# Hybrid attention step on one Trainium2 core: logits two heads ahead, exponentials one head ahead in a third buffer, and an index search that starts from mean and deviation

## What is computed

```python
s = einsum('bthd,bsd->bths', qi, ki)                    # 8 index heads of width 32
score = einsum('bth,bths->bts', wi, relu(s))
score = where(visible, score, -inf)                     # chunk-causal, chunks of 64
top_val, top_idx = lax.top_k(score, top_k)              # 256 prompt, 144 sample
logits = einsum('btjgd,btnjd->btjgn', qg, k_sel) * HEAD_DIM ** -0.5   # 8 heads
p = softmax(where(valid, logits, -inf)); o = einsum('btjgn,btnjd->btjgd', p, v_sel)
# memory: 4 heads over 256 memory tokens, softmax, values
```

## Time and profile before

| quantity | value |
|---|---|
| median of 3 runs (lowest to highest) | 3575.22 us (3574.49 to 3578.63) |
| the profiled execution's own time | 3577.81 us |
| its span, first to last instruction | 3576.0 us |
| mean granted TensorE clock over the span | 0.929 of full |
| busy over the span: PE, PEld, DVE, ACT, POOL | 3084.5, 2868.3, 2205.3, 1062.0, 1261.6 us |

### The profile page before, as it was taken

One profiled execution on the slowest core, in us unless ns is written; L12 is line 12 of the kernel. 1 busy time (PEld: TensorE's weight loads), 2 busy tenths in 40 slices (PEclk: granted clock), 3 DMA queues, 4 the chain that ended last, 5 costly groups with the idle time before them and its releaser, 6 DMA issues. The chain is left out here.

```text
span 3576.0 us, 49691 instructions
## 1 busy us (share of the span) xinstructions
PE 3084.5 (86%) x18810; PEld 2868.3 (80%) x18810; DVE 2205.3 (62%) x4136; ACT 1062.0 (30%) x1812; POOL 1261.6 (35%) x478
## 2 busy tenths in 40 slices
PE   3898994677778886886989999999888999999997
PEld 2777773566666775775989999999888999999996
DVE  4576672576868888863066666666512676667654
ACT  2222221444455664553122122112121212212211
POOL 0000001455666775411453343343214444434420
PEclk8999995688889997998989999999998999999998
DMA  4122225222121110003221111111132111111101
GB/s 137 70 81 78 89 84 138 56 57 57 29 57 29 29 29 26 23 14 99 78 71 36 35 59 47 35 47 47 49 103 89 36 47 59 35 35 59 47 12 50
DMA packets 164759, 201.53 MB, mean 56 GB/s; under 512 B 27759, under 2 KB 138644, under 8 KB 162580
## 3 DMA queue, kind: packets, MB, share of 16 engines
q1 hardware_dynamic: 164628, 199.86, 17.6%
HBM read 154.57 MB, written 45.25 MB: 56 GB/s over the span
## 5 line engine op out<-in xcount | busy, mean ns | idle before, releaser
L877 POOL TENSOR_TENSOR att_relu<-att_relu,keep_w 128x2048 f32<-128x2048 f32 (+12 forms) x84 | 255.5, 3041 | 923.0 <-ACT att_relu L1030 922.5
L1666 DVE SCALAR_TENSOR_TENSOR ffn_gv<-ffn_up,ffn_taps,ffn_gv 128x1056 f32<-128x1056 f32 (+2 forms) x264 | 417.7, 1596 | 143.0 <-ACT ffn_gv L1619 136.7
L1687 DVE TENSOR_TENSOR feed_hT<-feed_hT,ffn_ps_d 128x352 f32<-128x352 f32 x528 | 275.3, 522 | 328.4 <-PE ffn_ps_d L1572 328.4
L1559 PE MATMUL ffn_ps_u<-feed_nhi,feed_up_hi 128*128 128x352 f32 x2112 | 460.1, 326 | 15.9 <-DVE feed_nlo L1697 11.2
L1559 PE MATMUL ffn_ps_u<-feed_nhi,feed_up_lo 128*128 128x352 f32 x2112 | 456.7, 324 | 0.0
L1559 PE MATMUL ffn_ps_u<-feed_nlo,feed_up_hi 128*128 128x352 f32 x2112 | 456.0, 324 | 0.0
L1559 PEld LDWEIGHTS ffn_ps_u<-feed_nhi,feed_up_hi 128*128 128x128 f32 x2112 | 361.0, 190 | 19.7 <-DVE feed_nlo L1697 12.9
L1572 PE MATMUL ffn_ps_d<-ffn_a_hi,ffn_down_hi 128*128 128x352 f32 x1056 | 343.7, 326 | 29.3 <-DVE ffn_a_lo L1678 23.9
L1559 PEld LDWEIGHTS ffn_ps_u<-feed_nhi,feed_up_lo 128*128 128x128 f32 x2112 | 363.6, 188 | 0.0
L1559 PEld LDWEIGHTS ffn_ps_u<-feed_nlo,feed_up_hi 128*128 128x128 f32 x2112 | 360.0, 188 | 0.0
L1572 PE MATMUL ffn_ps_d<-ffn_a_lo,ffn_down_hi 128*128 128x352 f32 x1056 | 343.0, 325 | 0.0
(11 more groups left out here) (248 smaller groups left out, 6030.8 us busy)
## 6 DMA issues: line engine op xcount, KB each, us to landing
feed_raw_up<-in_w_up SPq DMA_DIRECT2D x44, 1024.0 KB, 5.0
scratch_sT<-proj_sT SPq DMA_DIRECT2D x16, 1472.0 KB, 5.1
ffn_raw_down<-in_w_down SPq DMA_DIRECT2D x22, 1024.0 KB, 4.9
feed_nlo<-scratch_mixT SPq DMA_DIRECT2D x16, 528.0 KB, 7.7
proj_x<-in_x_prompt SPq DMA_DIRECT2D x16, 512.0 KB, 4.7
att_qi<-scratch_sT SPq DMA_DIRECT2D x16, 512.0 KB, 3.8
att_qa<-scratch_sT SPq DMA_DIRECT2D x16, 512.0 KB, 5.0
att_qb<-scratch_sT SPq DMA_DIRECT2D x32, 256.0 KB, 5.6
```

Of the source, the lines that this page charges most:

```text
L877: st.step(pool.tensor_tensor(at, at, weights, ALU.mult))
L1559: ins = pe.matmul(ps_u[:, half, s, 0:SUB], a[:, q, k, :], b[:, k, SUB * s:SUB * s + SUB], start=(k == 0 and n == 0), stop=(k == KC - 1 and ...
L1666: ins = dve.scalar_tensor_tensor(gv[:, half, lo:hi], up[:, lo + shift + j - 2:hi + shift + j - 2], taps[:, 2 * j + half, e:e + 1], gv[:, h ...
L1687: dve.tensor_tensor(at, at, ps_d[:, j % 2, 0:SUB], ALU.add).then_inc(partial_read[j % 2], 1)
```

## The change

Logits and masked maxima are made two heads ahead of the head whose values are multiplied, instead of one; exponentials stay one head ahead, but now come first in ACT's slot instead of last, and `probs` has three buffers. PE no longer waits for the memory exponentials before the next block's logits: DVE copies the memory logits from PSUM to `probs`, and ACT works in place there. PE turns two groups before the first multiply, and the index pieces of a slot lie between the groups. The index pieces of a block are spread evenly over nine slots and start three slots earlier. The pick starts one slot earlier (in the last slot of the block before the previous one's end) and has 14 parts in eight slots; its threshold search starts at mean plus a tabled normal quantile times the deviation, and halves eight times from a step of 0.55 deviations, instead of eleven times from half of the range. In DVE's slot the divisions come before the masking. SP loads one more table.

```diff
-HALVINGS = 11
+HALVINGS = 8
+BRACKET = 0.55
+SQRT_SEED = 532487669.0
-        probs = m.sb("probs", [P, 2, SEQ])
+        probs = m.sb("probs", [P, 3, SEQ])
-        SHARE = 10
+        INDEX_LEAD = 3
+        SPREAD = ((0, 1), (2, 3), (4, 5), (6, 7), (8, 9), (10,), (11,), (12, 13))
+        def index_share(slot):
+            b = ahead(BLOCKS[0], (slot + INDEX_LEAD) // NHEADS + 2)
+            if b is None:
+                return None, []
+            total, part = IH * len(b.segs), (slot + INDEX_LEAD) % NHEADS
+            return b, list(range(total * part // NHEADS, total * (part + 1) // NHEADS))
+        def pick_share(slot):
+            b, part = ahead(BLOCKS[0], (slot + 1) // NHEADS + 1), (slot + 1) % NHEADS
+            return b, SPREAD[part] if b and part < len(SPREAD) else ()
...
+            sp.dma_start(quantiles[:, :], t["quantiles"]).then_inc(tables_loaded, 16)
             load(BLOCKS[1])
...
@@ segment_logits (PE)
-                if h == 0 and s < 2 and b.n:
-                    pe.wait_ge(exp_done, NHEADS * b.n)
@@ head_values (PE); rest holds the later segments of the head two ahead
-                turn(0)
+                for g in range(min(2, len(groups))):
+                    turn(g)
                 for g in range(len(groups)):
-                    if g + 1 < len(groups):
-                        turn(g + 1)
-                    if g == 0:
-                        index_pieces(other, numbers)
                     if rest:
                         segment_logits(*rest.pop(0))
                     ins = multiply(g)
+                    if g + 2 < len(groups):
+                        turn(g + 2)
+                    index_pieces(other, numbers[g:g + 1])
...
@@ the loop over slots (PE)
+            for slot in range(-INDEX_LEAD, 0):
+                index_pieces(*index_share(slot))
+            for first_heads in heads[0:2]:
+                early_logits(*first_heads)
+            for i, b, h, _, later in slots():
+                if later:
+                    early_logits(*later)
+                other, numbers = index_share(i)
+                index_pieces(other, numbers[0:2])
                 if h == 0 and b.n:
                     rows_turned(BLOCKS[b.n - 1])
-                head_values(b, h, other, late, after)
+                head_values(b, h, other, numbers[2:], later)
@@ exponentials (ACT), memory head
-                act.wait_ge(turned, last_group(seq - 2) + 1)
                 for mh in range(MH):
-                    ins = act.activation(probs[0:T, seq % 2, 256 * mh:256 * mh + 256], ps_l[...],
-                                         ACT.Exp, bias=neg[0:T, u, 8 + mh:9 + mh], accum_out=...)
+                    row = probs[0:T, seq % 3, MT * mh:MT * mh + MT]
+                    ins = act.activation(row, row, ACT.Exp, bias=neg[0:T, u, 8 + mh:9 + mh], accum_out=...)
@@ pick (DVE), part 0
-                    dve.tensor_reduce(col(low), row, AX.X, ALU.min)
-                    st.step(dve.tensor_reduce(col(mids), row, AX.X, ALU.max))
+                    dve.memset(col(mids), FAR)
+                    for s, (lo, hi) in enumerate(b.segs):
+                        last = dve.bn_stats(stats[0:T, s, :], row[:, lo:hi])
+                    st.step(last)
...
-                    st.step(dve.tensor_scalar(col(spread), col(mids), col(low), None, ALU.subtract))
-                    st.step(dve.tensor_scalar(steps[0:T, :], halves[0:T, :], col(spread), None, ALU.mult))
-                    st.step(dve.tensor_scalar(col(mids, 1), col(mids), col(steps), None, ALU.subtract))
+                    st.step(dve.bn_aggr(moments[0:T, :], stats[0:T, 0:len(b.segs), :].rearrange("p s n -> p (s n)")))
+                    st.step(dve.tensor_scalar(col(sigma).bitcast(I32), col(moments, 1).bitcast(I32), 0.5, SQRT_SEED, ALU.mult, ALU.add))
+                    st.step(dve.tensor_scalar(steps[0:T, :], halves[0:T, :], col(sigma), None, ALU.mult))
+                    st.step(dve.tensor_scalar(col(mids, 1), col(quantiles, b.n), col(sigma), col(moments), ALU.mult, ALU.add))
@@ mask_logits (DVE)
+                if part == 0 and seq >= 3:
+                    dve.wait_ge(turned, last_group(seq - 3) + 1)
...
+                    dve.tensor_copy(probs[0:T, seq % 3, 0:MH * MT].rearrange("p (a n) -> p a n", a=2), ps_l[0:T, :, :]).then_inc(masked, 1)
@@ the loop over slots (DVE)
+            pick(BLOCKS[1], 0)
+            for first_heads in heads[0:2]:
+                mask_logits(*first_heads, 0)
+            for i, b, h, _, later in slots():
                 if h == 0 and b.n:
                     divide(BLOCKS[b.n - 1], 2)
                 if h in (4, 8):
                     divide(b, h // GQ - 1)
+                coming, parts = pick_share(i)
+                if later:
+                    mask_logits(*later, 0)
+                for part in parts[0:1]:
+                    pick(coming, part)
+                if later:
+                    mask_logits(*later, 1)
+                for part in parts[1:]:
+                    pick(coming, part)
@@ constants; normal_quantile inverts the normal distribution on the host
-    halves = np.broadcast_to(f(0.5) ** np.arange(1, HALVINGS + 1, dtype=f), (P, HALVINGS))
+    halves = np.broadcast_to(f(BRACKET) * f(0.5) ** np.arange(HALVINGS, dtype=f), (P, HALVINGS))
+                quantiles[r, n] = normal_quantile(1 - (b.keep - 4.5) / seen)
```

More of the change, by code:

```diff
@@ L14 @@
+import math
 import numpy as np
@@ L947, in turn_group, with head_values @@
                 ins.then_inc(turned, 1)
-            def head_values(b, h, other, numbers, after):
+            def head_values(b, h, other, numbers, later):
                 u, T = b.n % 2, b.T
@@ L979, in multiply @@
                     return ins
-                rest = [(*after, s) for s in range(2, len(after[0].segs))] if after and after[1] < NH else []
-                turn(0)
+                rest = [(*later, s) for s in range(2, len(later[0].segs))] if later and later[1] < NH else []
+                for g in range(min(2, len(groups))):
+                    turn(g)
                 for g in range(len(groups)):
-                    if g + 1 < len(groups):
-                        turn(g + 1)
-                    if g == 0:
-                        index_pieces(other, numbers)
                     if rest:
@@ L1003, in _ @@
             pe.wait_ge(keys_loaded, 16 * KEY_LOADS)
-            early_logits(BLOCKS[0], 0)
-            for b, h, after in slots():
-                other = ahead(b, 2)
-                numbers = portion(other, h) if other else range(0)
-                late = numbers[-1:] if h else range(0)
-                if after:
-                    early_logits(*after)
-                index_pieces(other, numbers[:len(numbers) - len(late)])
+            for slot in range(-INDEX_LEAD, 0):
[7 more added lines that the diff above has]
+                index_pieces(other, numbers[0:2])
                 if h == 0 and b.n:
                     rows_turned(BLOCKS[b.n - 1])
-                head_values(b, h, other, late, after)
+                head_values(b, h, other, numbers[2:], later)
             rows_turned(BLOCKS[NB])
@@ L1047, in _, with relu_next @@
                 index_relu(b, range(IH * len(b.segs)))
-            exponentials(BLOCKS[0], 0)
-            for b, h, after in slots():
-                other = ahead(b, 2)
-                numbers = portion(other, h) if other else range(0)
-                early = len(numbers) - (1 if h and numbers else 0)
-                if other:
-                    index_relu(other, numbers[:early])
+            for slot in range(-INDEX_LEAD, 0):
+                index_relu(*index_share(slot))
+            exponentials(*heads[0])
+            for i, b, h, after, _ in slots():
+                if after:
+                    exponentials(*after)
                 if h == 0 and b.n:
                     copy_groups(act, BLOCKS[b.n - 1], 9)
-                copy_groups(act, b, h, (lambda: index_relu(other, numbers[early:])) if other else None)
-                if after:
-                    exponentials(*after)
+                other, numbers = index_share(i)
+                def relu_next(count, other=other or b, numbers=numbers):
+                    index_relu(other, numbers[:count])
+                    del numbers[:count]
+                copy_groups(act, b, h, relu_next)
             copy_groups(act, BLOCKS[NB], 9)
@@ L1228, in _ @@
                     divide(b, h // GQ - 1)
-                if h < 8 and not b.sample:
-                    pick(ahead(b, 1), 2 * h)
-                if after:
-                    mask_logits(*after, 1)
-                if h < 8 and not b.sample:
-                    pick(ahead(b, 1), 2 * h + 1)
+                coming, parts = pick_share(i)
[7 more added lines that the diff above has]
+                    pick(coming, part)
             divide(BLOCKS[NB], 2)
@@ L1820, in program, with normal_quantile @@
         store_conv(nc, t, ident, hist)
+def normal_quantile(share):
```

(5 more changed lines are left out.)

64 lines of the change are left out of this document (30 added, 34 removed).

## The result

| | before | after |
|---|---|---|
| median of 4 runs each, us | 3576.07 (3574.49 to 3578.63) | 3515.06 (3512.60 to 3517.95) |
| profiled execution, span | 3577.81, 3576.0 | 3515.56, 3513.8 |
| blocks 1 to 14 of the attention | 912.1 | 852.0 |

The ratio is 0.983 (95% interval 0.9818 to 0.9842): 61 us faster, where 115 were forecast. The time is 55 us above the forecast and nearer to the 3525 that the port rule gave. It lies inside the 3392 to 3530 that was to hold 8 in 10, but 5 us beyond the forecast's own 3415 to 3510: only the part of the range that was borrowed from rival 2 holds it.

A forecast was written before the change was run, and what follows sets the result against it. Inner slots were taken as bound by DVE with PE 4% behind, the rest lost at block edges. The terms summed to -115 us from 3577.8, less 2.6 for the median: 3460 us, 8 in 10 within 3392 to 3530.

The forecast's parts named there:

- the port rule: Each mask write on DVE could lose one whole GpSimd instruction at the shared port: 84 us instead of 19, sum 3525.
- rival 2: Two `ps_l` banks keep PE's edges as long as now and POOL's wait half becomes PE's: 3547 us, chance 0.16.
- three halvings: Three fewer threshold halvings in each of 15 blocks, in DVE slots without a gap, taken whole: -92 us.
- start of the pick: On DVE, two reductions go, while statistics per segment and two small steps per block come: net -11 us.
- memory copy: 17 DVE copies of 128x1024 from PSUM to SBUF, priced at the like-shaped mask instruction: +21 us.
- wait for POOL's scores: At block starts, earlier index pieces remove most of DVE's 68.1 us wait, about 10 kept: -58 us.
- edges -28: At block edges, DVE's 56.4 us of waits for PE's logits are halved: -28 us.
- what takes the place +60: Engines share slots less evenly, PE stalls at unit 0; some 4 us come back per block over 15: +60 us.
- blocks 0, 15, 16: Half of the few idle stretches in the last two blocks saved, nothing in the first: -7 us.
- POOL beside DVE: Mask writes already lose 19 us beside POOL; its larger share of time adds 3, left in the range.
- The first: Engines fit better, nothing comes back and waits at edges vanish: 3362, more likely 3375 to 3400 us; chance 0.15.
- The third: A threshold misses its bracket, so blocks run `take_largest`, 91 us each; two such blocks give 3620 us; chance 0.03.

The follow-up runs named there:

- quarters: Changed kernel with each POOL weighting and first sum split into four instructions and the second sum into two: 3467.80 us.
- values first: Changed kernel with each group's multiplies on PE put ahead of the held logit segment: 3506.50 us; with POOL's instructions also cut, 3453.79.
- the search one part later, the fastest run: Changed kernel with POOL's instructions cut, multiplies ahead of held logits, and the search's parts moved by one place: 3444.86 us.

## Why the prediction was off by half

| term | forecast, us | measured, us | from |
|---|---|---|---|
| three halvings | -92 | -90 | L1110 and its small steps and reads, 322.6 to 232.6 |
| start of the pick | -11 | -14 | reductions 41.0 out; statistics, aggregate and root 26.9 in |
| memory copy | +21 | +21 | 17 at 1.213 |
| wait for POOL's scores | -58 | -67 | 68.1 to 0.6 |
| waits for PE: edges -28, what takes the place +60 | +32 | +51 | 56.4 to 107.8 |
| blocks 0, 15, 16 | -7 | 0 | +6, -6, 0 |
| POOL beside DVE | 0, 3 in the range | +40 | 23 to 63 |
| sum | -115 | -59 | profiled executions: -62 |

The measured column adds up because VectorE's busy time and its waits fill the stretch. It says where the time stands; what caused it is for the runs to show.

**Right.** 120 halvings at the old price; the wait for POOL gone; none on the memory exponentials; statistics at 606 ns (22.1 us against 24); three extra mask writes; the inner heads h = 1 to 3 of block 11 still at 6.9 us. Two signs failed: block 11 at 67 us (76.8), and h = 0, which takes 9.5 us with DVE waiting 2.6 of them for PE. That the earlier index pieces take POOL's wait away is shown by undoing them (+60).

**The step that failed** is "POOL beside DVE": "POOL's share of the stretch would rise from 59% to about 67% (536 over 800), which adds 3; I leave that in the range". I scaled the old loss with POOL's share of the time, and took the mask write as the only instruction concerned. In the trace it is a meeting of single instructions: what counts is which of DVE's stand beside which of POOL's, and the change moved both. The marking, for which the prediction has no port price at all, gave 19 of the 40 (26.1 to 45.4), the write 17, an eight-column step 4. Cutting POOL's instructions shows it: 30 and 51 us off the port, 33 and 47 off the time, the whole miss but 8 (11 of the 51 are what the kernel before lost already). That the marking pays could have been read in the trace of before, by single shapes: 1408 columns took longer than 1536.

```profile
L1106 DVE SCALAR_TENSOR_TENSOR att_work<-att_work,att_scores 128x1408 f32<-128x1408 f32 x1 | 3.2, 3206 | 0.0
L1106 DVE SCALAR_TENSOR_TENSOR att_work<-att_work,att_scores 128x1536 f32<-128x1536 f32 x1 | 1.8, 1754 | 0.0
```

The Trainium skill (SBUF — State Buffer, Who interferes with whom) covers the marking too, "A DVE instruction with two SBUF inputs contends with a GpSimd instruction that reads SBUF", and says the form with an accumulator does not. The trace agrees with both: 1.741 to 3.029 for the one, and 1.431 before and after for the halvings. I had read the rule for the mask write only, and then left its 3525 outside the sum and without a chance of its own.

**The term that was mis-sized** is the waits for PE, +51 for +32. The runs do not put it down to the port: with quarters PE's waits behind masks fall from 138 to 99 us, but VectorE's waits for PE stay, at 109.6. Each half of the change alone raises them as much: over 600 to 1700 us these waits are 128 us before and 184 after, 192 with the new search spread in the old order, and 202 with the old search in the new order. They fall with PE's order and the layout of the search: 96.5 in blocks 1 to 14 with quarters and values first, 78.7 with the search one part later as well. The waits with quarters alone:

```profile
DVE att_probs L1221 <- PE att_ps_l L946: 76.2, 62, 4.6
DVE att_inv L1231 <- PE att_ps_o L994: 19.0, 10, 3.6
DVE att_neg L1209 <- PE att_ps_l L932: 14.4, 14, 2.2
```

So the -28 and +60 together were too small by 19, and no run takes apart what that hangs on. In block 11 the working also left out the second mask of h = 7 (1.08 us at 1217.04). One bound is off and enters nothing else: by the row that it names, the low end of the copy is 10 and not 12.

**Luck in the sum.** "They stand in slots where DVE has no gap, so I take them whole" came out at -90 as busy time, but the halvings are not worth that by themselves. In the old order the same search gave +28 or -29 according to its layout. The terms are bound to one another, and a sum of them holds for the whole change only. That 3515 fell inside the range is luck in part: the room came from rival 2, and most of it was filled by the port.

**The rivals.** The second (two PSUM banks keep the edges) forecast 3547, and its sign came true: PE's wait behind masks rose by 54 us, past the 52.6. But the quarters, which leave the banks as they are, take 47 of the 55 us back. How much of the waits for PE that stay hangs on the banks is open, since no run gives `ps_l` more of them. The first (nothing takes the place, 3375 to 3400) is not reached even by the fastest run, 3445. The third did not occur: the mask was written 18 times, as before.

## What to carry to other kernels

Before an instruction is moved beside work on GpSimd, list which of VectorE's instructions take the shared port (here a mask write from SBUF to SBUF and one with two SBUF inputs), and price each at the rest of the GpSimd instruction that it may meet, not at a share of the time. Long GpSimd instructions are then a cost for VectorE: cut in four they cost 62 us more on GpSimd and took 47 off the time, but only in the order in which GpSimd had slack; where it was on the path, the same edit lost 12. And test the halves of a change apart: here the order alone lost 70 us, the search alone lost 28 or gained 29 by its layout over the slots, and both together gained 61.

## What the runs showed that I had not expected

An instruction of eight columns waits as well as one of 1664: the step at L1106 took 1.64 us at 1223.53 in block 11, where it takes 0.23 with quarters. It ended at 1225.17, when POOL's weighting did.

```profile
1221.76 3.39 POOL L889 TENSOR_TENSOR att_relu<-att_relu,keep_w 128x1920 f32<-128x1920 f32 x1 [8.17 <-ACT att_relu L1042]
...
1223.53 1.64 DVE L1106 TENSOR_SCALAR att_steps<-att_halves,att_sigma 128x8 f32<-128x8 f32 x1
```

And POOL pays as well: its second sum of 896 columns took 2.09 us undisturbed, 3.62 behind the marking and 2.74 behind the mask write.

PE's own time fell without fewer matmuls: 695.3 us before, 649.0 after, 624.0 in the fastest run, at a mean granted clock of 0.86, 0.90 and 0.95. Right behind the stall of 2.12 us that ended at 1191 the clock was 0.66 over 5 us, between its two levels of 1.2 and 2.4 GHz (0.5 and 1), and it was 1.00 over the undisturbed 1160 to 1180. The eight transposes there took 1.91 us instead of 1.04, so at this place PE lost more than the length of its stall. No term of the prediction had that, and no run takes it apart from the stalls.
